# First chunk of the forget projection ahead of the transposes of the third token tile

## The reference

```python
h = concat([meta_tokens, x])                       # (1040, 1024)
u = rmsnorm(h, g_pre)
qa, ka, va, za, qf, kf, vf, zf, ff, ga, gf = split(u @ w_in)
y_swa = swa_branch(qa, ka, va, sinks) * silu(za)   # window of chunks, ALiBi, sinks
log_f = log_sigmoid(ff + b_forget)                 # (1040, 8)
y_fox = fox_branch(qf, kf, vf, log_f) * silu(zf)   # causal, decay = cumsum(log_f)
merged = sigmoid(ga + b0) * (y_swa @ w_up_swa) + sigmoid(gf + b1) * (y_fox @ w_up_fox)
out = (h + rmsnorm(merged @ w_out, g_post))[16:]
```

## Time and profile before

| | us |
|---|---|
| median of three runs | 849.58 (848.36 to 851.98) |
| the profiled execution | 849.09 |
| its span in the trace | 847.2 |
| PE busy | 804.2 (95%) |
| DVE busy | 502.9 (59%) |
| POOL busy | 350.6 (41%) |
| ACT busy | 315.2 (37%) |

### The profile page before, as it was taken

The page is one execution under the profiler, slowest core; times in us unless marked ns, Lnnn a source line. Parts: engine busy times, 40 slices in busy tenths (PEclk is TensorE's granted clock), DMA queues, the critical chain, the costliest instruction groups (busy, mean ns, idle before and its releaser), DMA issues.

```text
span 847.2 us, 12887 instructions
## 1 busy us (share of the span) xinstructions
PE 804.2 (95%) x4514; PEld 649.7 (77%) x4514; DVE 502.9 (59%) x1050; ACT 315.2 (37%) x645; POOL 350.6 (41%) x292
## 2 busy tenths in 40 slices
PE   3999989999999999999999989799998999999996
PEld 3999989988878878788788855566665688878885
DVE  7944788256776777645646347485878844442222
ACT  6432241333333333333333236365676323222111
POOL 4412214354435435444344325556785444412221
PEclk9999999999999999999999999799999999999999
DMA  9341425369857346365364598996900375443221
GB/s 291 103 125 52 127 64 133 91 168 265 242 163 204 111 139 196 95 173 169 95 182 111 140 231 216 240 245 140 243 3 2 109 238 149 125 163 111 95 79 74
DMA packets 121795, 124.99 MB, mean 148 GB/s; under 512 B 29970, under 2 KB 91874, under 8 KB 121732
## 3 DMA queue, kind: packets, MB, share of 16 engines
q1 hardware_dynamic: 120292, 119.92, 52.3%
q10 hardware_dynamic: 1440, 4.26, 1.3%
HBM read 90.93 MB, written 34.92 MB: 149 GB/s over the span
## 4 chain that ended last, share of the span: by engine, by line
PE 81%; DVE 9%; DMA 3%; issue 3%; ACT 2%; SPq 1%; POOL 1%; DVEq 0%; ACTq 0%; POOLq 0%
PE PS L1837 18%; PE PS L1838 18%; PE PS L1839 18%; PE PS L2084 3%; PE PS L2086 3%; PE PS L2085 3%; PE PS L2007 3%; PE PS L1944 2%; DVE t_val L1589 2%; DMA VF<-v_dram 2%; PE PS L1987 2%; PE PS L1988 1%; PE PS L2022 1%; PE PS L2037 1%; DVE t_lo L1597 1%
## 5 line engine op out<-in xcount | busy, mean ns | idle before, releaser
L1140 POOL TENSOR_TENSOR ops<-s_sum,ops 128x512 fp32r<-128x512 f32 x64 | 87.4, 1376 | 114.3 <-ACT ops L1238 114.3
L1837 PE MATMUL PS<-t_hi,ops 128*128 128x512 f32 x256 | 101.1, 395 | 0.0
L1838 PE MATMUL PS<-t_lo,ops 128*128 128x512 f32 x256 | 99.8, 390 | 0.0
L1839 PE MATMUL PS<-t_hi,ops 128*128 128x512 f32 x256 | 99.8, 390 | 0.0
L1140 POOL TENSOR_TENSOR ops<-raw,ops 128x512 fp32r<-128x512 f32 x48 | 65.0, 1355 | 69.8 <-ACT ops L1238 69.7
L1209 POOL TENSOR_TENSOR acc<-acc,p_fox 128x400 f32<-128x400 f32 (+5 forms) x76 | 62.2, 839 | 5.9 <-ACT p_fox L1362 3.6
L1161 POOL TENSOR_TENSOR w_plain<-raw,w_plain 128x1024 fp32r<-128x1024 f32 x10 | 28.0, 2804 | 85.3 <-ACT w_plain L1267 85.3
L1668 DVE TENSOR_TENSOR z_tmp<-u,PS 128x512 f32<-128x512 f32 x48 | 33.0, 687 | 48.9 <-PE PS L1839 28.2
L1362 ACT ACTIVATE p_fox<-PS,neg_c_col 128x512 f32<-128x512 f32 (+5 forms) x112 | 54.1, 534 | 21.1 <-PE PS L1993 15.8
L1238 ACT ACTIVATE ops<-s_sum 128x512 fp32r<-128x512 f32 x64 | 39.6, 624 | 54.9 <-DVE s_sum L1470 41.1
L1839 PEld LDWEIGHTS PS<-t_hi,ops 128*128 128x128 f32 x256 | 48.1, 188 | 10.6
(11 more groups left out here) (203 smaller groups left out, 2198.9 us busy)
## 6 DMA issues: line engine op xcount, KB each, us to landing
raw<-in_w_in_dram SPq DMA_DIRECT2D x34, 512.0 KB, 5.2
q_dram<-stage_b SPq DMA_DIRECT2D x32, 256.0 KB, 3.1
g_dram<-stage_b SPq DMA_DIRECT2D x32, 256.0 KB, 2.0
tanh_g<-g_dram SPq DMA_DIRECT2D x16, 512.0 KB, 4.2
max_k<-k_dram SPq DMA_DIRECT2D x16, 260.0 KB, 5.3
max_c<-neg_c_dram SPq DMA_DIRECT2D x8, 520.0 KB, 6.5
x_all<-in_x_dram SPq DMA_DIRECT2D x8, 512.0 KB, 7.7
raw<-in_w_in_dram SPq DMA_DIRECT2D x16, 256.0 KB, 4.6
```

Source lines behind the costliest of these rows:

```text
L1140: nc.gpsimd.tensor_tensor(ops[:, i % OPS, 1], op_source(p, name), ops[:, i % OPS, 0].bitcast(F32), ALU.subtract).then_inc(op_ready, 1)
L1837: pe.matmul(dst, hi_w, hi, start=first, stop=False)
L1838: pe.matmul(dst, hi_w, lo, start=False, stop=False)
L1839: return pe.matmul(dst, lo_w, hi, start=False, stop=last)
```

## The change

The forget chunk of column group 0 is handed to turn 3 and not to turn 4.

```diff
     early = {m: [] for m in range(NQ + 4)}
     for c in range(4):
         for x in range(3):
-            early[4 + 2 * c + (x + 1) // 2].append((x, c))
+            early[3 if x + c == 0 else 4 + 2 * c + (x + 1) // 2].append((x, c))
```

## The result

The changed kernel takes 852.91 us (median of 8 runs, 851.71 to 854.45), the kernel before 848.75 us in the runs beside it (8 runs, 846.79 to 851.98). The ratio is 1.0043, 95% interval 1.0030 to 1.0057: slower, though by less than the 0.5% that was set as the bound of "no change"; the median is 0.1 us above the forecast of 852.8. The profiled execution took 854.45 us, 849.09 before.

A forecast was written before the change was run, and what follows sets the result against it. PE was taken as the bound, with DVE's chain beside it almost without slack from tile 6 on. 4.6 us later minus 0.9 gained back gives 3.7; 849.09 + 3.7 = 852.8 us, range 850.3 to 855.0.

The forecast's parts named there:

- The wait: PE ahead of the moved chunk: waits for tile 2's low part until about 19.3, idle 1.3 to 1.4 us more.
- Chunk and transposes: On PE: chunk takes 3.6 us to 22.9, tile 3's transposes about 1.5 us to 24.4, clock rising at 24.2.
- The second copy: ACT's copy of the second half of tile 3's high part: starts 4.6 us later, near 24.5.
- late bound: ACT's second copy if PE's clock rises late: 5.0 us later, not 4.6.
- DVE held by POOL: L1455 and the scaling of tile 5 stay held by POOL's work and shift by 4.6 us; scaling ends near 32.0.
- rival that one of them comes free: New timing frees L1455 of tile 5 or tile 6's scaling from POOL: 851.0 us for one, 849.1 both; chance 0.15.
- What is gained back: Forget drain leaves its place between tile 5's scaling and tile 6's `u_var` on DVE, hidden in a wait: 0.88 us.
- The sum: DVE's lateness from tile 6 on reaches PE: 4.6 − 0.9 = 3.7 us, giving 852.8 us.
- late clock: Upper bound of the sum if PE's clock rises late: 5.0 − 0.9 = 4.1 us.
- PE's own loss: The part of the lateness at the chunk behind tile 7 due to PE itself: only about 1.2 us.
- rival of a clock that falls again: PE's 2.0 us of idle pieces between 28 and 37 us lower its clock: about 855 at worst; chance 0.20.
- sign of being wrong: One of the listed signs: PE late at 44 us and no longer late at 100 us.

The follow-up runs named there:

- b: Changed kernel with both halves of the low part of tile 2 ahead of the scaling of tile 3 on DVE; 851.01 us, ratio 1.0015.
- h: Changed kernel with 16 extra identity transposes on PE ahead of the moved chunk; 851.93 us, ratio 1.0021.
- g: Kernel before with 12 extra identity transposes on PE ahead of the transposes of tile 3; 849.33 us, ratio 0.9991.
- d: Changed kernel with ACT's and POOL's split of the second key weight ahead of the copies of tile 3; 851.89 us, ratio 1.0015.
- k: Kernel before with every gain multiplied in on DVE and none on POOL; 847.69 us, ratio 0.9972.
- a: Changed kernel with the first forget chunk's drain back at its old place behind the scaling of tile 5; 854.19 us, ratio 1.0056.
- m: Changed kernel with every gain on DVE and none on POOL; 848.58 us, ratio 0.9991 to the kernel before.
- c: Kernel before with both halves of the low part of tile 2 ahead of the scaling of tile 3 on DVE; 849.75 us, ratio 0.9995.
- i: Changed kernel with the low part of tile 2 ahead of the scaling of tile 3, plus 9 identity transposes ahead of the moved chunk; 848.98 us, ratio 0.9985.
- l: Kernel before with no gain on POOL, plus 8 identity transposes on PE ahead of those of tile 3; 846.87 us, ratio 0.9959.
- f: Kernel before with the gain of tile 4 taken from POOL to DVE; 848.15 us, ratio 0.9977.

## Why the prediction held

**The wait.** PE would wait for the low part of tile 2, until 19.3, with 1.3 to 1.4 us more of idle time. It did: 19.27 (19.47 − 0.20), and 4.52 − 3.11 = 1.41. The 0.1 us for the first weights was an estimate that no row of the kernel before shows; in the trace after, 0.14 us of issue stand between the end of L1514 at 19.33 and the chunk. b shows that this wait is a cause: without it 3.1 of the 4.05 us are gone, 0.94 of them by the clock.

**Chunk and transposes.** Chunk until 22.9, transposes 1.5 us, end at 24.4. Measured, less 0.20: 23.08, 1.72 and 24.80. The mis-sized term is the rise of the clock, taken as a middle value at 24.2; it came at about 24.8, as the granted clock shows (from:to, length, busy of PE, weight loads, DVE, ACT, POOL, then granted clock, DMA share, GB/s):

```profile
14.00:18.00 4.00, 0.94 (x5) 0.60 (x3) 3.97 (x5) 2.52 (x5) 4.00 (x3) 1.00 1.12 343
18.00:22.00 4.00, 2.53 (x12) 1.77 (x13) 3.18 (x8) 1.24 (x3) 2.28 (x1) 0.52 0.92 232
22.00:26.00 4.00, 4.00 (x24) 3.72 (x23) 1.68 (x4) 1.57 (x3) 0.00 (x0) 0.63 1.08 281
26.00:30.00 4.00, 3.85 (x31) 3.62 (x30) 3.24 (x5) 2.67 (x6) 3.35 (x2) 1.00 0.46 110
```

The granted clock read 0.52 over 18 to 22 us; over single microseconds it read 0.50 from 19 to 24, 0.51 over 24 to 25 and 1.00 over 25 to 26. The 0.63 of 22 to 26 us is 3.0 us at 0.5 and 1.0 us at 1.00, so the rise is at 25.0, less 0.20. h shows the price of the low clock in the new order: 2.4 us. In the old order it is 0.3 (g).

**ACT.** The second copy 4.6 us later, at most 5.0. Measured 25.03 − 0.20 − 19.93 = 4.90, near the late bound, for the reason just named.

**DVE held by POOL.** L1455 and the scaling of tile 5 would be held as before. They were, 2.18 and 2.70 us, and the scaling ended at 32.47 − 0.20 = 32.27, 4.9 late. The rival that one of them comes free didn't happen; d shows what a free L1455, an earlier root and a sooner clock are worth together: 2.7 us. L1455 took 2.18 us beside POOL's split and 0.22 us without it (0.22 in d, and at 29.13 before). Which of the two starts first goes with this in the traces: a scaling with the gain in it, L1506, that started at 11.51, ahead of POOL's gain at 12.06, took 1.28 us, and the one that started at 24.65, behind POOL's gain at 23.89, took 2.72. In k, L1506 at 19.25 took 1.28 us too, ahead of POOL's split at 19.67. The rows of before at 11.51 and 12.06 (two gains in one row):

```profile
11.51 1.28 DVE L1506 SCALAR_TENSOR_TENSOR x_all<-x_all,stat,g_pre_row 128x1024 f32<-128x1024 f32 x1
12.06 5.26 POOL L1168 TENSOR_TENSOR x_all<-x_all,g_pre_row 128x1024 f32<-128x1024 f32 x2 [1.37 <-ACT squares L1274]
```

**What is gained back.** 0.88 us from the drain. In the trace 0.85 (4.9 of lateness at tile 5, 4.05 at the PE point); a measured 0.63, and 0.85 with its sooner clock added.

**The sum.** 4.6 − 0.9 = 3.7 was predicted and 4.9 − 0.85 = 4.05 came. That the median lies only 0.1 us from the forecast is in part luck: the forecast stood on an execution of 849.09 us, the kernel before had a median of 848.75 beside the change, and the step between the medians was 4.2, above the 4.1 of the late clock. PE's own loss was put at 1.2 and DVE's lateness at the rest; m gives 1.6 for the first. The rival of a clock that falls again in PE's new gaps, which has the chance 0.20 and the upper end of the range, didn't come: the gaps were 0.15, 0.77 and 0.48 us, and eight transposes behind the last of them, at 36.89, took 1.09 us, not 1.97. What such a fall would add there is an estimate that no run shows. The trace of before has one far from this part: PE busy for 0.63 us of 576 to 578, then a granted clock of 0.76 and 0.50, and four microseconds at their mean of 0.63 would cost PE 1.5 us.

**After 45 us.** The same PE instruction is 4.24 us later in the changed kernel's trace at 45 us and still at 100 us (100.04 before, 104.29 after), 4.02 us later from 107 to 470 us, and between 3.2 and 5.4 us later behind 500 us, 5.4 at the end. So the sign of being wrong, late at 44 us and no longer at 100, didn't show. What changes behind 500 us is a difference between executions: the control c, which isn't late at 45 us, lies there between 1.16 us ahead of the kernel before and 1.06 behind it. The medians differ by 4.2.

## What to carry to other kernels

Where engines share one order of steps, moving a step forward on PE puts all that waits behind it at the mercy of the moved step's inputs: ask first when the last of them is ready, by the order of the engine that makes it, and then who waits for what was overtaken. Here 1.4 us more of idle time and the chunk of 3.6 us came ahead of the transposes of tile 3, and 4.05 us of it stayed, because those transposes fed ACT, then POOL, then a DVE without slack. And ask of any help that POOL gives DVE what it holds up: here giving all the gains back to DVE was worth 0.3%, with a chain of DVE work that PE waits for.

## What the runs showed of the hardware

**Behind a fill the clock was up.** The sixteen identity transposes of h took 2.14 us in all, and behind a further 2.55 us of idle time the sixteen matmuls of the chunk ran at 0.124 us each (19.43 to 21.41). With the change alone, without the fill, they ran at 0.226 (19.47 to 23.08). In each of four pairs of profiled executions the first instructions behind the wait ran at the low pace without the fill and at the full one with it: the change and h, b and i (0.42 and 0.29 us for the first matmul), before and g, k and l (1.97 and 1.09 us for eight transposes).

**It can also be up without a fill, and fall during work.** In f PE had no fill. The transposes of tile 3 ran at the full pace at 16.70 (1.09 us for eight), behind 1.72 us of idle time, and then the granted clock fell:

```profile
18.00:22.00 4.00, 3.96 (x20) 3.04 (x21) 3.90 (x7) 3.14 (x6) 3.04 (x2) 0.57 0.91 223
```

It is 0.57 over these 4 us, with PE busy for 3.96 of them. In the kernel before eight transposes at 17.92 took 1.97 us: the same PE work ahead of them, but 3.11 us of idle time, and the clock not up. The length of the idle time alone doesn't tell: in k it was 0.99 us, and the eight transposes behind it, at 15.96, took 1.97 us too. And over 18 to 22 us of the kernel before the granted clock reads 1.00 though twelve matmuls ran at 0.225 us: in this first stretch the level has to be read from durations.

```profile
18.00:22.00 4.00, 4.00 (x19) 3.28 (x20) 3.86 (x10) 3.76 (x8) 2.55 (x2) 1.00 0.86 201
```

In the changed kernel the granted clock falls at about 18 us, while PE is idle (1.00 over 17 to 18, 0.58 over 18 to 19, 0.50 over 19 to 20). Whether the clock had risen shortly before, as in f, or was low all along, can't be told: PE does nothing there.
